# A two-layer block with expert lookup: the last two query tiles' chunks alternate, and table rows are gathered into memory freed by them

## What is computed

```python
def peer_ffn(h, wq, keys, u_tab, v_tab):
    q = (ht @ wq).reshape(n, PEER_HEADS, 2, PEER_DK // 2)            # 256 x 8 x 2 x 128
    s = jnp.einsum('nhpc,pkc->nhpk', q, keys)                        # 128 keys each
    s1, i1 = lax.top_k(s[:, :, 0], PEER_TOPK)                        # 16
    s2, i2 = lax.top_k(s[:, :, 1], PEER_TOPK)
    cand = (s1[..., :, None] + s2[..., None, :]).reshape(n, PEER_HEADS, 256)
    sc, ci = lax.top_k(cand, PEER_TOPK)
    e = take(i1, ci // 16) * N_KEYS + take(i2, ci % 16)
    gate = jax.nn.softmax(sc, axis=-1)
    a = einsum('nd,nhkd->nhk', x, u_tab[e])                          # 128 rows of u_tab per token
    w = gate * gelu(a)
    return einsum('nhk,nhkd->nd', w, v_tab[e])                       # 128 rows of v_tab per token
```

## Time and profile before

| | us |
|---|---|
| median of 3 runs (lowest, highest) | 3048.84 (3047.76, 3050.46) |
| the profiled execution's own time | 3049.02 |
| its span | 3047.1 |
| DVE busy | 2462.3 (81%) |
| PE busy | 2106.5 (69%) |
| POOL busy | 652.1 (21%) |

### The profile page before, as it was taken

How to read it: one execution, slowest core, us unless ns; L and a number is a source line. 1 busy time by engine, 2 the same in 40 slices (tenths; PEclk the granted TensorE clock), 3 DMA queues, 4 the chain that set the end, 5 groups by cost and what they waited for, 6 DMA issues and landing times.

```text
span 3047.1 us, 24729 instructions
## 1 busy us (share of the span) xinstructions
PE 2106.5 (69%) x8570; PEld 1583.4 (52%) x8570; DVE 2462.3 (81%) x2627; ACT 886.3 (29%) x931; POOL 652.1 (21%) x656
## 2 busy tenths in 40 slices
PE   9999999999999999999998910004565200016562
PEld 7888888888888887788787810001122100002121
DVE  6675689999999987575565899979998899986677
ACT  5544443333333365534454411110000000000000
POOL 0000000000000000000000075863333343333332
PEclk9999999999999999999999955557767655557866
DMA  6454778898988955344354599999999999999997
GB/s 246 173 199 169 300 262 321 328 346 333 337 334 329 350 216 180 139 153 155 125 207 153 215 405 397 417 422 421 421 422 421 422 422 422 422 422 421 421 421 313
DMA packets 133191, 958.52 MB, mean 315 GB/s; under 512 B 14833, under 2 KB 15153, under 8 KB 17137
## 3 DMA queue, kind: packets, MB, share of 16 engines
q0 software_dynamic: 89824, 650.98, 52.4%
q1 hardware_dynamic: 43280, 306.44, 27.2%
q10 hardware_dynamic: 2, 0.01, 0.0%
HBM read 955.23 MB, written 2.13 MB: 314 GB/s over the span
## 4 chain that ended last, share of the span: by engine, by line
PE 56%; DMA 24%; DVE 14%; issue 3%; POOL 2%; ACT 1%; SPq 0%; DVEq 0%; POOLq 0%; ACTq 0%
DMA rows_g<-in_v_tab_dram,idx 18%; PE bank L641 17%; PE bank L645 17%; PE bank L642 17%; DVE rows_g L2620 9%; DMA rows_g<-in_u_tab_dram,idx 5%; PE bank L1165 2%; POOL rows_g L618 2%; DVE bank L2669 1%; DMA raw<-in_wstream_dram 1%; PE bank L673 1%; PE bank L994 0%; PE bank L940 0%; PE bank L681 0%; DVE WL L1774 0%
## 5 line engine op out<-in xcount | busy, mean ns | idle before, releaser
L1774 DVE TENSOR_TENSOR WL<-raw,WH 128x2048 fp32r<-128x2048 f32 x287 | 656.9, 2290 | 290.9 <-ACT WH L1179 284.9
L1165 PE MATMUL bank<-rows_g,diag 128*128 128x512 f32 x488 | 350.8, 886 | 735.4 <-DMA rows_g<-in_v_tab_dram,idx 735.4
L641 PE MATMUL bank<-WH,UH 128*128 128x512 f32 x1952 | 772.3, 396 | 5.8 <-DVE WL L1774 2.7
L645 PE MATMUL bank<-WH,UL 128*128 128x512 f32 x1952 | 762.7, 391 | 0.0
L642 PE MATMUL bank<-WL,UH 128*128 128x512 f32 x1952 | 762.4, 391 | 0.0
L1179 ACT ACTIVATE WH<-raw 128x2048 fp32r<-128x2048 f32 x287 | 549.8, 1917 | 685.9 <-DMA raw<-in_wstream_dram 672.5
L1165 PEld LDWEIGHTS bank<-rows_g,diag 128*128 128x128 f32 x488 | 134.3, 289 | 952.6 <-issue 649.5
L2620 DVE CUSTOM_DVE_ANT_0 rows_g<-rows_g,bank 128x2048 f32<-128x2048 f32 x233 | 524.5, 2285 | 35.0 <-DMA rows_g<-in_u_tab_dram,idx 34.3
L2669 DVE SCALAR_TENSOR_TENSOR bank<-rows_g,gate_w,bank 128x2048 f32<-128x2048 f32 x193 | 454.5, 2355 | 117.5 <-DMA rows_g<-in_v_tab_dram,idx 99.1
L641 PEld LDWEIGHTS bank<-WH,UH 128*128 128x128 f32 x1952 | 367.8, 188 | 83.1 <-issue 5.9
L645 PEld LDWEIGHTS bank<-WH,UL 128*128 128x128 f32 x1952 | 367.9, 188 | 77.2
(11 more groups left out here) (402 smaller groups left out, 1621.7 us busy)
## 6 DMA issues: line engine op xcount, KB each, us to landing
raw<-in_wstream_dram SPq DMA_DIRECT2D x288, 1024.0 KB, 4.8
ada_w<-in_ada_dram POOLq DMA_DIRECT2D x96, 1024.0 KB, 7.3
rows_g<-in_u_tab_dram,idx POOLq DMA_INDIRECT x256, 23.4
rows_g<-in_v_tab_dram,idx POOLq DMA_INDIRECT x256, 30.4
X<-in_x_dram SPq DMA_DIRECT2D x4, 512.0 KB, 9.8
c_row<-in_c_rows_dram POOLq DMA_DIRECT2D x1, 2048.0 KB, 8.8
ctx_x<-in_ctx_dram POOLq DMA_DIRECT2D x1, 2048.0 KB, 10.2
gb<-mod_rows POOLq DMA_DIRECT2D x2, 1024.0 KB, 5.8
```

Source lines behind the costliest of these rows:

```text
L641: pe.matmul(o, ah[:, k0 + k, t], wh[:, w], start=first and k == 0, stop=False)
L645: mm = pe.matmul(o, al[:, k0 + k, t], wh[:, w], start=False, stop=last and k == nk - 1)
L1165: mm = pe.matmul(bank[c], diag[:, n % 2, :], row(q)[:, c * CW:(c + 1) * CW], start=s == mine[0], stop=s == mine[-1])
L1774: dve.tensor_tensor(WL[:, n % SLOTS_W, :], raw[:, n % SLOTS_W, :], WH[:, n % SLOTS_W, :].bitcast(F32), ALU.subtract).then_inc(lo_ready, 1)
```

## The change

1. The weights of query tiles 2 and 3 are streamed in turn, a chunk of tile 2, a chunk of tile 3, both with the same input rows; PE fills both PSUM pairs side by side. Their turns and key products come behind the last chunk on PE, and on ACT and DVE both copies come at the end.
2. As the input's first 1024 rows are used up after 12 of the 16 chunks, buffers 2 and 3 lie there (places 0 and 2); the other buffers move up by two.
3. The first two gathers wait for the indices and for `xn2_ready`, no longer for a chunk.
4. `choose` does the finish in one piece with s = 1, and DVE's three first dots and the piece behind them stand ahead of both copies.

```diff
-ROW_AT = (14, 15, 4, 8, 5, 9, 6, 10, 7, 11, 0, 1, 2, 3)
-ROW_CHUNK = (0, 0, 1, 1, 2, 2, 3, 3, 4, 4, 4, 4, 4, 4)
+ROW_AT = (14, 15, 0, 2, 4, 8, 5, 9, 6, 10, 7, 11, 1, 3)
+ROW_CHUNK = (None, None, 0, 0, 1, 1, 2, 2, 3, 3, 4, 4, 4, 4)
@@ GpSimd, before each gather
                     if q < GATH:
-                        if not ROW_CHUNK[q]:
+                        if ROW_CHUNK[q] is None:
                             pool.wait_ge(sem("xn2_ready"), NB)
-                        pool.wait_ge(split_used, NCH - SLOTS_W + ROW_CHUNK[q])
+                        else:
+                            pool.wait_ge(split_used, NCH - SLOTS_W + ROW_CHUNK[q])
@@ TensorE
+            def tile_pair(n, q, work):
+                for m in range(CPT):
+                    for j in range(2):
+                        if m == 0:
+                            pe.wait_ge(acc_free_act, q + j + 1)
+                            pe.wait_ge(acc_free_dve, q + j + 1)
+                        products(n + 2 * m + j, ACC[(q + j) % 2], m * CK, CK, None, 0, UH, UL, first=m == 0, last=m == CPT - 1)
+                        next(work, None)
+                for _ in work:
+                    pass
...
                 for t in range(OUT_TILES):
-                    yield from until(CPT * (t + 1))
+                    yield from until(CPT * (t + 1) if t < 2 else CPT * OUT_TILES)
...
-                    yield from until(CPT * (t + 1) + 1)
+                    yield from until(CPT * (t + 1) + 1 if t < 2 else 0)
...
-            linear_among(S_WQ, Q_WQ, 0, OUT_TILES, queries(), ready=u_parts(4, 1))
+            asked = queries()
+            linear_among(S_WQ, Q_WQ, 0, 2, islice(asked, 2 * CPT), ready=u_parts(4, 1))
+            tile_pair(S_WQ + 2 * CPT, Q_WQ + 2, asked)
@@ ScalarE: queries() as on TensorE, and
-            linear_among(S_WQ, Q_WQ, 0, OUT_TILES, to_q, queries())
+            asked = queries()
+            linear_among(S_WQ, Q_WQ, 0, 2, to_q, islice(asked, 2 * CPT))
+            for m in range(2 * CPT):
+                hi(S_WQ + 2 * CPT + LEAD + m)
+                next(asked, None)
+            for t in (2, 3):
+                act.wait_ge(split_used, NCH + t - 3)
+                to_q((Q_WQ + t) % 2, t)
+            for _ in asked:
+                pass
@@ VectorE: to_q
-                if t == OUT_TILES - 1:
-                    next(begun, None)
-                    for q in range(FIRST_ROWS):
-                        dot(0, q, XN2[:, 0, :])
-                    next(begun, None)
-                    dve.wait_ge(split_used, NCH)
@@ VectorE: choose
-                    yield
+                    if s == 0:
+                        yield
...
                 dve.tensor_copy(idx[:, b, mine], pick_f[:, :]).then_inc(sem("idx_ready"), 1)
+                yield
@@ VectorE: the last two tiles
-            linear_among(S_WQ, Q_WQ, 2, OUT_TILES, to_q, islice(begun, 2 * CPT), work_first=True)
+            for m in range(2 * CPT):
+                next(begun, None)
+                lo(S_WQ + 2 * CPT + LEAD + m)
+            next(begun, None)
+            for q in range(FIRST_ROWS):
+                dot(0, q, XN2[:, 0, :])
+            next(begun, None)
+            for t in (2, 3):
+                dve.wait_ge(split_used, NCH + t - 3)
+                to_q((Q_WQ + t) % 2, t)
@@ host: layout of the stream
-    put(S_WQ, chunks(first["peer_wq_2"]))
+    asked = chunks(first["peer_wq_2"])
+    put(S_WQ, asked[:2])
+    put(S_WQ + 2 * CPT, asked[2:].swapaxes(0, 1))
```

More of the change, by code:

```diff
@@ L1695, in queries @@
                 for t in range(OUT_TILES):
-                    yield from until(CPT * (t + 1) + 1)
+                    yield from until(CPT * (t + 1) + 1 if t < 2 else CPT * OUT_TILES)
                     for j in range(2):
@@ L1700, in queries @@
                                        ACT.Copy).then_inc(sem("q_t_ready"), 1)
-                    yield from until(CPT * (t + 1) + 2)
+                    yield from until(CPT * (t + 1) + 2 if t < 2 else 0)
                     for b in range(NB):
```

## The result

Over 9 runs each, the changed kernel takes 3058.17 us (3054.88 to 3062.98) and the kernel before 3049.72 us (3047.76 to 3052.6): 8.5 us slower, a ratio of 1.0029 with a 95% interval of 1.0021 to 1.0037. The profiled execution took 3058.17 us with a span of 3056.3. 3050.4 had been forecast, with a range up to 3055.0, so the time lies outside it, on the side of rival D.

What follows compares the result with a forecast made beforehand. VectorE's dots and choices were taken to bound the kernel up to 1920 us, DMA from there to the end. The terms 0 + 0 + 0 + 4.5 - 3.1 = +1.4 us on 3049.02 gave 3050.4 us, range 3042.5 to 3055.

Steps and rivals of the forecast that it cites:

- rival D: Query stage: gathers hold up the last chunk's load, 10 us instead of 4.7; 3055.7 us, chance 0.11.
- The bound: Up to 1860 us: a microsecond VectorE gains or loses in its first table moves the end by about as much.
- The gathers: Query stage: first indices and gathers come 7 us sooner; booked 0, as rows fetched ahead of VectorE stand in buffers.
- PE: End of the chunks: PE's last chunk ends 2.5 us sooner, at 1756.8 us; worth 0 by itself.
- The streamed chunks: Last chunk's load: a delay up to 1.3 us is hidden, third dot ends at 1759.98 as before; 0.
- DVE's tail: Behind the third dot: copies come 5.6 us late, ScalarE and PE wait, fourth dot at 1777.8 us; cost 4.5 us.
- The regained hit: DVE's CAST of 1790.83 us falls between two POOL multiplies and is not held; gain 3.1 us.
- DMA dry: From 1780 us DMA runs dry for some microseconds; booked 0, as 17 rows have landed by then.

Runs made afterwards that it cites:

- b1_first_late: The kernel before with its first two gathers held back by one more chunk; +0.1 us against the kernel before, ratio 1.0001.
- n2_before_slots: The kernel before with the choices' pieces of block 0 behind slots 1, 3 and 7 of every 12, not 3, 7 and 11; -4.6 us, ratio 0.9985.
- m1_copies_first: The changed kernel with both DVE query copies ahead of the s = 1 piece and finish; +3.0 us against the kernel before, ratio 1.0007.
- m2_hold_gathers: The changed kernel with the third gather also waiting until the stream's last chunk has landed; +10.5 us against the kernel before, ratio 1.0028.
- n1: The changed kernel with ScalarE's sum of row 3 moved ahead of its copy into PSUM; +7.6 us against the kernel before, ratio 1.0022.
- n4_combined: The changed kernel with VectorE's and ScalarE's tail reordered and the choices' pieces behind slots 1, 3, 7 of 12; -6.8 us against the kernel before, ratio 0.9970.
- p2_multiply_later: n4_combined with POOL's first multiply behind the fourteenth gather, not the twelfth; 3039.79 us, 9.9 us faster than the kernel before, ratio 0.9967.
- n3_after_slots: The changed kernel with the choices' pieces behind slots 1, 3 and 7 of every 12; +0.9 us against the kernel before, ratio 1.0003.
- p3_slots_hold: n3_after_slots with the third gather held until the last chunk has landed; +0.2 us against the kernel before, ratio 1.0004.
- b2: The kernel before with only the early first indices and first two gathers, order of copies, dots and tiles kept; +2.4 us, ratio 1.0007.

## Why the prediction was wrong, by its own steps

- **The bound** held in this order of work: "when VectorE gets through its first table" decides. b1_first_late shows no value of early rows, n2_before_slots a gain from DVE alone. But a microsecond of DVE moves the end "by about as much" only until DMA's own loss is used up: there 12.1 us of dots gave 4.6.
- **The gathers**, 7 us sooner: measured 7.2. Booked 0, and worth 0 as long as DVE leads.
- **PE** 2.5 us sooner: measured 2.7.
- **The streamed chunks: 0. This step failed.** I took a delay up to 1.3 us as hidden and the third dot "as before". The load took 9.9 us, not 4.7, and the low part and the third dot came 3.5 us late. The 1.3 us that the copy and the finish free lie ahead of the low part, where DVE now stood 6.39 us for the load; from the low part to the first dot it takes 9.8 us in both kernels, so nothing there could hide a delay. Rival D had exactly these two numbers, with a chance of 0.11, and then took 1.3 us off that the 3.5 already had in it.
- **DVE's tail: +4.5.** The fourth dot came 7.9 us late: the 3.5 of the load and 4.4 of the tail. The mechanism and the size held; m1_copies_first gives 7.1 us back by the place of the copies alone, more than the tail's own 4.4, since its tail is 2.7 us shorter than even that of the kernel before (10.6 us for 13.3 from the third dot's end to the fourth dot): the wait of 2.03 us for the copy into PSUM is gone and the hold costs 1.2 us less (3.28 for 4.50), against 0.6 for the second copy.
- **The regained hit: -3.1.** Measured 3.05, the CAST took 0.19 us. It hangs on the time of the third multiply: in m1, m2 and n1 the hit came back.
- **DMA dry: 0. This term was too low, but little.** "17 rows have landed by then" was right, and the first 68 dots wait for no row. POOL's stall of 12.65 us put DMA 6.7 us behind at +100; most of that is what VectorE's late dots cost anyhow, and at +240 there are 5.7 us for dots 4.8 us late. So the term measures 0.9 us by what DMA moved, 2.2 by the profiled end and 3.6 by the noisy medians.
- The sum with measured terms is 3.5 + 4.4 - 3.05 = 4.8 on the dots, as measured, and with 0.9 for DMA 5.7, its lag. The profiled execution ends 7.0 us late from tile 1's copy, and the medians say 8.5 (6.4 to 11.3). What makes up the rest, 1.3 to 2.8 us, is not shown; in most of the profiles the end comes some 1 us later than the lag says, so the kernel before's own profiled execution may have ended early by as much.
- **The range** ended at 3055.0, under the 3055.7 of rival D itself. With the delay in full (3.5 + 4.5), the regained hit and 0.9 for DMA the forecast would have been 5.8 over 3049.02, or 3054.8, and a range that reached as far above it as this one did above 3050.4, 4.6 us, would have held the 3058.17. That D's own 3055.7 came within 2.5 us of the time is in part luck: it left out the regained hit (3.1 us too much), DMA's share (0.9 too little) and took 1.3 off, which nearly cancel.

## What to carry to other kernels

Where an engine that hands out buffers is the pace, starting transfers early buys nothing, and what the early transfers disturb (the last loads of the stream before) is paid in full. The early start pays once that engine is out of the way, as in n4_combined and p2_multiply_later: 3.5 and 5.8 us of transfers beyond n2_before_slots. Look at what stands behind a moved copy on the other engines, and give it first place: here copies of 0.7 us that stood behind a held piece kept ACT and PE waiting, and through ACT's sum the one row buffer behind which all of POOL's gathers stood. And booking a dry DMA at nothing needs a look at the point where the pace changes: what is still lost there, beyond what the slower engine costs anyhow, is owed until the end. It helps to count what DMA had moved by that point, from a step that both kernels share: that set apart n4_combined and p2_multiply_later, or n3_after_slots and p3_slots_hold, by some 2.4 us, where their ratios agree.

## What the runs showed of the hardware that I had not expected

- A load of 1 MB, from its issue to ScalarE's start on it, took 4.7 us with two gathers issued 2.1 us and more behind it, 4.9 with none near (b1), 7.3 to 7.7 with two gathers issued before it (p3, b2, m2) and 9.9 with two before and two behind. The queues show how: q0 has the gathers, q1 the load (packets, MB, share of the DMA engines' time). In the change, for 3 us from the load's issue at 1737.29, then the next 3, then up to 1747.19:

```profile
q0 software_dynamic: 167, 1.24, 98.9%
...
q1 hardware_dynamic: 97, 0.79, 62.4%
q0 software_dynamic: 78, 0.51, 40.3%
...
q0 software_dynamic: 191, 1.43, 86.9%
q1 hardware_dynamic: 47, 0.25, 15.6%
```

  Nothing of the load moves in the first 3 us, while the two rows ahead of it go (2.1 MB, of which 0.56 had moved before the load's issue); then it shares with the rest of them and the two rows behind it. Before, 0.60 MB of it moved in the first 3 us, and in m2_hold_gathers none in the first 3, then all of it in the next 4.7. I had cited the Trainium skill ("DMA: Bandwidth & Descriptors", on arbitration) for a load that does not wait out all gathers. The trace bears out turns for the rows behind the load, but not for those ahead of it.
- A gather's issue takes 0.94 us. Where it begins within one of DVE's two-input operations from SBUF (low part or dot with XN2, 2.29 us), it ends 0.80 to 0.89 us after that operation, in all 57 such issues that the 13 profiles have between 1700 and 2010 us, whether the issue then takes 1.1 us or 2.8; dots with one operand in PSUM don't hold it. The inference in "SBUF — State Buffer", section "Who interferes with whom", of the Trainium skill was that such an operation leaves the writing of descriptors alone. The trace doesn't refute that as it stands, since a gather also reads its indices from SBUF, and the wait may be that read's; but in this case a gather's issue is held by such an operation all the same. The rule on the read interface in that section of the Trainium skill agrees with the multiply, which waited 1.1 us for the third dot. DVE's small operations waited for the multiply in turn.
- The holds come at fixed places while POOL follows DVE: 3.22 to 3.26 us behind slots 23, 35 and 47 in every profile that has pieces there. Behind slot 11, where the phase of the two still differs, it is 3.24 or 3.25 in five profiles, 4.71 in m2, 5.19 in m1 and none in the change. With the pieces behind other slots all of them vanish.
